# A fourth split slot and later dependent steps in the expert-pair loop of a two-layer transformer trunk

## The reference

```python
logits = (t @ w_router + b_router).astype(jnp.float32)
top_vals, top_idx = lax.top_k(logits, TOP_K)
top_w = jax.nn.softmax(top_vals, axis=-1)
combine = ...                                   # (tokens, 8), two weights per row
for e in range(N_EXPERTS):
    out = out + combine[:, e:e+1] * swiglu(t, w_gate[e], w_up[e], w_down[e])
# swiglu(x) = (silu(x @ w_gate) * (x @ w_up)) @ w_down
# w_gate, w_up: 1024 x 3584, w_down: 3584 x 1024 for each of the 8 experts, all float32
```

## Time and profile before

| | before |
|---|---|
| profiled execution | 1546.36 us |
| its span, first to last instruction | 1544.5 us |
| median of three runs | 1546.59 us |
| PE busy | 1405.0 us (91%) |
| DVE busy | 1282.1 us (83%) |
| ACT busy | 961.6 us (62%) |
| mean DMA rate over the span | 303 GB/s |
| chain that ended last | PE 65%, DVE 16%, issue 10%, ACT 7%, DMA 1% |

### The profile page before, as it was taken

One profiled execution on the slowest core, in us unless ns is written; L12 is line 12 of the kernel. 1 busy time (PEld: TensorE's weight loads), 2 busy tenths in 40 slices (PEclk: granted clock), 3 DMA queues, 4 the chain that ended last, 5 costly groups with the idle time before them and its releaser, 6 DMA issues.

```text
span 1544.5 us, 19314 instructions
## 1 busy us (share of the span) xinstructions
PE 1405.0 (91%) x7122; PEld 1150.3 (74%) x7122; DVE 1282.1 (83%) x1182; ACT 961.6 (62%) x935; POOL 5.6 (0%) x36
## 2 busy tenths in 40 slices
PE   2999799999998699999999999989999998999995
PEld 2877699998877477777777777777777777777774
DVE  6976798886777688889879889888899888898986
ACT  1644443333454367777767777767777777777773
POOL 0000000000000000000000000000000000000000
PEclk9987899998999899999999999999999999999998
DMA  8962389984540489999979999988999988999980
GB/s 332 346 246 83 136 290 342 334 304 164 182 167 1 168 305 370 377 380 377 381 281 354 380 385 375 388 305 311 383 386 382 382 332 296 373 380 385 379 337 29
DMA packets 203949, 467.44 MB, mean 303 GB/s; under 512 B 8734, under 2 KB 10940, under 8 KB 203836
## 3 DMA queue, kind: packets, MB, share of 16 engines
q1 hardware_dynamic: 203836, 465.98, 81.9%
HBM read 464.90 MB, written 1.05 MB: 302 GB/s over the span
## 4 chain that ended last, share of the span: by engine, by line
PE 65%; DVE 16%; issue 10%; ACT 7%; DMA 1%; SPq 0%; DVEq 0%; ACTq 0%
PE bank L1564 16%; PE bank L1566 16%; PE bank L1565 16%; DVE w_lo L1346 10%; ACT w_hi L722 5%; PE bank L1969 3%; PE bank L1886 1%; DVE ring_sum L960 1%; PE bank L1585 1%; PE bank L1607 1%; PE bank L1951 1%; PE bank L1950 1%; PE bank L1895 1%; PE bank L1764 1%; PE bank L1993 1%
## 5 line engine op out<-in xcount | busy, mean ns | idle before, releaser
L1346 DVE TENSOR_TENSOR w_lo<-raw,w_hi 128x2048 fp32r<-128x2048 f32 x336 | 755.8, 2288 | 86.5 <-ACT w_hi L722 86.5
L722 ACT ACTIVATE w_hi<-raw 128x2048 fp32r<-128x2048 f32 x336 | 637.8, 1921 | 143.9 <-PE bank L1566 102.8
L1564 PE MATMUL bank<-w_hi,hg_hi 128*128 128x512 f32 x448 | 183.1, 409 | 19.4 <-DVE w_lo L1346 17.7
L1950 PE MATMUL bank<-w_hi,gs_pack 128*128 128x512 f32 x448 | 180.7, 403 | 10.8 <-DVE w_lo L1346 9.4
L540 ACT ACTIVATE w_hi<-raw 128x2048 fp32r<-128x2048 f32 (+1 forms) x54 | 102.3, 1897 | 130.8 <-PE bank L1566 117.0
L1565 PE MATMUL bank<-w_lo,hg_hi 128*128 128x512 f32 x448 | 177.8, 397 | 0.0
L1566 PE MATMUL bank<-w_hi,hg_lo 128*128 128x512 f32 x448 | 177.7, 397 | 0.0
L1951 PE MATMUL bank<-w_lo,gs_pack 128*128 128x512 f32 x448 | 175.5, 392 | 0.0
L889 DVE TENSOR_TENSOR w_lo<-raw,w_hi 128x2048 fp32r<-128x2048 f32 (+1 forms) x54 | 121.7, 2258 | 19.4 <-ACT w_hi L540 19.2
L1564 PE MATMUL bank<-h_hi,w_hi 128*128 128x256 f32 x448 | 128.2, 286 | 1.6 <-DVE gate_m L938 1.6
L1565 PE MATMUL bank<-h_lo,w_hi 128*128 128x256 f32 x448 | 126.7, 283 | 0.0
(11 more groups left out here) (302 smaller groups left out, 2113.4 us busy)
## 6 DMA issues: line engine op xcount, KB each, us to landing
raw<-in_w_ex_gate SPq DMA_DIRECT2D x112, 1024.0 KB, 6.5
raw<-in_w_ex_up SPq DMA_DIRECT2D x112, 1024.0 KB, 7.2
raw<-in_w_ex_down SPq DMA_DIRECT2D x112, 1024.0 KB, 6.4
raw<-in_w_ada SPq DMA_DIRECT2D x48, 1024.0 KB, 7.2
raw<-in_w_in SPq DMA_DIRECT2D x12, 1024.0 KB, 7.0
raw<-in_w_ff_gate SPq DMA_DIRECT2D x10, 1024.0 KB, 6.5
raw<-in_w_ff_up SPq DMA_DIRECT2D x10, 1024.0 KB, 7.0
raw<-in_w_ff_down SPq DMA_DIRECT2D x10, 1024.0 KB, 6.5
```

What stands on the lines that cost most here:

```text
L722: act_e.activation(w_hi[:, (S0 + n) % SPLIT, :], raw[:, (N0 + n) % RAW, :], ACT.Copy).then_inc(hi_done, 1)
L1346: dve.tensor_tensor(w_lo[:, sl, :], raw[:, (N0 + n) % RAW, :], w_hi[:, sl, :].bitcast(F32), ALU.subtract).then_inc(lo_done, 1)
L1564: mm(o, lh, rh, start=first, stop=False, skip_group_check=True)
L1950: mm(bank[b][:, :], gs_pack[:, kk, :], wh[:, k, :], start=kk == 0, stop=False, skip_group_check=True)
```

## The change

What it does:
- The pair loop gets a fourth slot for `w_hi` and `w_lo` (`more_hi`, `more_lo`, PAIR_SPLIT = 4); the buffers that stood in their place move, `e_hi`, `e_lo` and `f_pack` become single.
- After the router, PE transposes the modulated `hfm` back to token-major rows and ACT writes them over `y` (`modulated_rows`, four copies of 128x512). The gathers then bring rows that are modulated already; ACT takes their high part in one instruction from PSUM (`hg_hi` per half, `gs_pack` at once) and DVE the remainder in one, from PSUM too. `hgf`, `gsf` and the casts go.
- `silu_l(c+1)` and `silu_s(c)` move behind L down half 0 and `gated_s` too, `gated_l` behind S gate half 0, `high_l`, `keep_gate` and `low_l` behind S down half 0, `keep_up` behind the first unit of the next chunk.
- The transposed `e_act` goes to bank 1 in place of bank 0, so that L gate of the next chunk waits for `silu_l` alone and L up for the split; the selection goes to bank 0, a chunk later, and `select` a chunk earlier (chunks 2 and 3).
- ACT at unit n waits for the use of unit n-4.

```diff
-    SEL_L, SEL_S = 3, 4
+    SEL_L, SEL_S = 1, 2
+        pair_hi = [w_hi[:, i, :] for i in range(SPLIT)] + [more_hi[:, :]]
+        pair_lo = [w_lo[:, i, :] for i in range(SPLIT)] + [more_lo[:, :]]
...
+            def modulated_rows():
+
+                for i in range(4):
+                    g, half = i // 2, i % 2
+                    act_e.wait_ge(ym_tp, i + 1)
+                    act_e.activation(y[:, g, half * 512:(half + 1) * 512], bank[i][:, :], ACT.Copy).then_inc(ym_done, 1)
...
                 act_e.wait_ge(hgl_ready, n * 2 + (half + 1))
-                for k in range(4 * half, 4 * half + 4):
-                    modulated(hgf[:, k, :], bank[1 + 2 * half][:, (k % 4) * P:(k % 4 + 1) * P], k, hglf_done)
+                act_e.activation(hg_hi[:, 4 * half:4 * half + 4, :],
+                                 bank[3 * half][:, :].rearrange("p (k t) -> p k t", t=P), ACT.Copy).then_inc(hgl_high, 1)
...
                 act_e.wait_ge(hgs_ready, n + 1)
-                for k in range(KD):
-                    modulated(gsf[:, k, :], bank[3][:, k * HALF:(k + 1) * HALF], k, hgsf_done)
+                act_e.activation(gs_pack[:, :, 0:HALF], bank[3][:, :].rearrange("p (k t) -> p k t", t=HALF),
+                                 ACT.Copy).then_inc(hgs_high, 1)
...
-                    hi_of(j, p * (16 * PU // RAW) + 16 * ((N0 + j) // RAW + 1), p * PU + (S0 + j - SPLIT + 1))
+                    hi_of(j, pair_hi[j % PAIR_SPLIT], p * (16 * PU // RAW) + 16 * ((N0 + j) // RAW + 1),
+                          p * PU + (S0 + j - PAIR_SPLIT + 1))
...
-                    if u[0:2] == ("L", "up") and half == 1:
-                        if c > 0:
-                            silu_s(c - 1)
-                        silu_l(c)
                     if u == ("L", "up", 0, 1):
+                        silu_l(0)
                         evacuate_s(p)
-                    if u == ("L", "gate", 1, 1):
+                    if u == ("S", "up", 0, 1):
+                        keep_gate(0)
+                        high_l(0)
+                    if u == ("L", "gate", 1, 0):
                         keep_up(0)
...
+                    if u[0:2] == ("L", "down") and half == 0 and c < LAST:
+                        silu_l(c + 1)
+                        silu_s(c)
+                    if u[0:2] == ("S", "down") and half == 0 and c < LAST:
+                        keep_gate(c + 1)
+                        high_l(c + 1)
...
+                    if u[0:2] == ("L", "gate") and half == 0 and c > 1:
+                        keep_up(c - 1)
+                    if u == ("S", "down", LAST - 1, 1):
+                        evacuate_l(p + 1, 0)
+                        keep_up(LAST)
...
-                    if u[0:2] == ("L", "down") and half == 1 and c + 1 < EC:
-                        gated_l(c + 1)
-                    if u[0:2] == ("L", "up") and half == 1 and c > 0:
-                        gated_s(c - 1)
-                    if u[0:2] == ("S", "up") and half == 1:
-                        low_l(c)
-                    if u == ("S", "up", LAST, 1):
+                    if u[0:2] == ("S", "gate") and half == 0 and c > 0:
+                        gated_l(c)
+                    if u[0:2] == ("L", "down") and half == 0 and c < LAST:
+                        gated_s(c)
+                    if u == ("S", "up", 0, 1):
+                        low_l(0)
+                    if u[0:2] == ("S", "down") and half == 0 and c < LAST:
+                        low_l(c + 1)
+                    if u == ("S", "down", LAST - 1, 1):
                         split_l(p + 1, 0)
...
+            def rows_of(i):
+
+                g, half = i // 2, i % 2
+                for k in range(4):
+                    last = pe.transpose(bank[i][:, k * P:(k + 1) * P], hfm[:, 4 * half + k, g * P:(g + 1) * P], ident[:, :])
+                last.then_inc(ym_tp, 1)
+
+            rows_of(0)
+            rows_of(1)
             pe.wait_ge(lgt_done, 1)
...
                     if c > 0:
-                        pe.wait_ge(elo_done, p * EC + c)
+                        pe.wait_ge(esilu, p * EC + c)
...
-                    if c == 1:
-                        pe.wait_ge(tl_done, p * 2 + 2)
-                    if c == 2:
-                        pe.wait_ge(ts_done, p * 2 + 2)
+                    if c > 0:
+                        pe.wait_ge(elo_done, p * EC + c)
                     into_l("up", c, 1)
```

More of the change, by code:

```diff
@@ L27 @@
 SPLIT = 3
+PAIR_SPLIT = 4
 UNIT = 2048
@@ L222, in trunk_kernel @@
         late = ExitStack()
[L223 to L228, removed]
+        more_hi = sb("more_hi", [P, UNIT], F32R, where=late)
+        more_lo = sb("more_lo", [P, UNIT], F32R, where=late)
         late.close()
@@ L247, in trunk_kernel @@
         sin2 = sb("sin2", [P, G, 1, RO])
+        summed = ExitStack()
+        g_pre = sb("g_pre", [P, 512], where=summed)
+        u_pre = sb("u_pre", [P, 512], where=summed)
+        summed.close()
         ring_sum = sb("ring_sum", [P, 2, 512])
@@ L295, in trunk_kernel @@
         e_act = sb("e_act", [P, 512], where=moe)
-        e_hi = sb("e_hi", [P, 2, 4, P], F32R, where=moe)
-        e_lo = sb("e_lo", [P, 2, 4, P], F32R, where=moe)
-        hgf = sb("hgf", [P, KD, P], where=moe)
+        e_hi = sb("e_hi", [P, 4, P], F32R, where=moe)
+        e_lo = sb("e_lo", [P, 4, P], F32R, where=moe)
+        f_act = sb("f_act", [P, 4, HALF], where=moe)
+        f_pack = sb("f_pack", [P, 4, P], F32R, where=moe)
+        gs_pack = sb("gs_pack", [P, KD, P], F32R, where=moe)
         hg_hi = sb("hg_hi", [P, KD, P], F32R, where=moe)
@@ L842, in rest_of_expert @@
                             act_e.wait_ge(x_hg_ready, q * 2 + (i + 1))
-                            for k in range(4 * i, 4 * i + 4):
-                                modulated(hgf[:, k, :], bank[6 + i][:, (k % 4) * P:(k % 4 + 1) * P], k, x_hgf)
+                            act_e.activation(hg_hi[:, 4 * i:4 * i + 4, :],
+                                             bank[6 + i][:, :].rearrange("p (k t) -> p k t", t=P), ACT.Copy).then_inc(x_high, 1)
                     if u == ("gate", 0, 1):
@@ L1885, in gather_l @@
                     for g in range(G):
[L1886 removed]
+                        last = mm(bank[3 * half][:, (k % 4) * P:(k % 4 + 1) * P], y[:, g, k * P:(k + 1) * P], sel[:, g, :],
                                   start=(k % 4 == 0 and g == 0), stop=g == 1, skip_group_check=True)
@@ L1945, in into_s @@
                         wh, wl = unit(("S", kind, c, half))
-                        if (kind, c) == ("gate", 0):
-                            pe.wait_ge(hgs_done, p * 4 + (2 * half + 2))
+                        if (kind, c, half) == ("gate", 0, 0):
+                            pe.wait_ge(hgs_done, p + 1)
                         for k in range(4):
@@ L1980, in down_l @@
                                 cs = slice(half * 512, (half + 1) * 512)
-                                last = product(bank[4 + half][:, :], e_hi[:, c % 2, kk, :], e_lo[:, c % 2, kk, :],
+                                last = product(bank[4 + half][:, :], e_hi[:, kk, :], e_lo[:, kk, :],
                                                wh[:, k, cs], wl[:, k, cs], c == 0 and kk == 0, c == LAST and kk == 3)
@@ L1992, in down_s @@
                                 cs = slice(half * 512, (half + 1) * 512)
-                                mm(bank[6 + half][:, :], f_pack[:, c % 2, kk, :], wh[:, k, cs], start=c == 0 and kk == 0,
+                                mm(bank[6 + half][:, :], f_pack[:, kk, :], wh[:, k, cs], start=c == 0 and kk == 0,
                                    stop=False, skip_group_check=True)
-                                last = mm(bank[6 + half][:, :], f_pack[:, c % 2, kk, :], wl[:, k, cs], start=False,
+                                last = mm(bank[6 + half][:, :], f_pack[:, kk, :], wl[:, k, cs], start=False,
                                           stop=c == LAST and kk == 3, skip_group_check=True)
```

122 lines of the change are left out of this document (55 added, 67 removed).

## The result

| | before | after |
|---|---|---|
| median | 1546.48 us (4 runs, 1540.57 to 1547.13) | 1490.17 us (4 runs, 1486.86 to 1493.57) |
| profiled execution, its span | 1546.36, 1544.5 us | 1490.64, 1488.9 us |
| ratio of the times | | 0.9646 (95%: 0.9625 to 0.9668) |

The kernel is 3.5% faster, 56 us. The forecast was 1474 with 1464 to 1515 as the range: the sign and the larger part of the size came as said, 16 us of the gain are missing. The time lies inside the range but above the forecast's own (A, 1464 to 1486), between it and rival B (1500).

The account below looks back on a forecast made before the run. Chunks took 33.2 us, above the PE, DVE and DMA limits, through slot waits, plus boundary stops. DMA-paced landings (unit 331 at 1429), last split at 1446.5, 24.0 us tail and router's 1.1 gave span 1471.6, forecast 1474, range 1464 to 1515.

Parts of the forecast that it names:

- A: Main forecast: DMA sets the pace between boundaries and boundaries shorten; 1474 us, own range 1464 to 1486, chance 0.54.
- rival B: Raw slots don't carry the lag, or PE's clock falls at times; DMA stops at each pair boundary: 1500 us, chance 0.22.
- Three limits, chunk at PE's 30.1 us, then DMA's 32.4: Steady chunk, now 33.2 us: engines alone would need PE's 30.1, so DMA's 32.4 takes over, giving 0.8 us a chunk.
- The fourth slot's lead of 4.2 against 2.9 us: On L units four slots give 4.2 us lead, three give 1.4; PE gains 2.9 on DVE in the S half.
- They add no work: Later steps, other banks and single buffers in the lists: claimed to add no work, with silu_s no longer stopping ACT.
- Gathers, 2.5 to 0.6 us on the path: At gather_s, ACT's copies on the path shrink from 2.5 to 0.6 us; DVE drops four casts per pair.
- Boundary, 53.1 us: Step-by-step walk of the pair boundary: 17 units take 53.1 us instead of 61.3, 8.2 us less.
- The raw slots carry a lag of up to 9.7 us: At boundaries the seven raw slots keep the DMA queue fed up to 9.7 us lag; up to 8 is needed.
- Router, +1.1 us: Ahead of the loop, PE's transposes and ACT's four copies add between 0 and 1.6 us on the path; 1.1 taken.
- Rival D: DMA is at its limit already, by contention with the engines; only trifles stay, 1542 to 1550 us, chance 0.08.
- Rival C: Fourth slot doesn't even out L and S; chunk stays at 33.2 us, only boundaries gain: 1514 us, chance 0.10.
- Rival E: PE standing at S units lowers its clock, each fall costing 1.7 us; three falls a chunk give 1610 us, chance 0.06.

## Why the prediction came out as it did

*Three limits, chunk at PE's 30.1 us, then DMA's 32.4: right.* Behind a boundary the chunks are 30.4 to 30.9, at the end of a pair 31.9. DMA's limit was set 1.7% too slow: my 2.705 us a unit came from a window of 40 us ahead of the experts, while in the loop gate and up units land 2.71 us apart and down units 2.56, 2.66 on average, 31.9 us for 12.

*The fourth slot's lead of 4.2 against 2.9 us: right, but not enough by itself.* Without the later places the slot gave 14 us. The step that failed in the text is "They add no work": a step that makes ACT wait for PE takes from the same 4.2 us. I had costed ACT's stops at nothing because the ledger was one of work. Before had one at the fold in every chunk, 69.3 us in all, where after has 23.4:

```profile
ACT f_act L781 <- PE bank L1969: 69.3, 28, 2.6
```

The forecast's total held only because both parts were made together.

*Gathers, 2.5 to 0.6 us on the path: not seen.* With PE's jump in the kernel the difference is none. It is still part of the walk that came out at 53.1, but no run isolates it there.

*Boundary, 53.1 us: the failed step.* It says "L gate 0 at 14.7": PE starts the next pair as soon as its unit is split. PE stands 4.45 us at the jump and then runs 3.4 to 6.8 us at half clock, which costs half of that: 4.45 + 3.4 = 7.9 at the first boundary, 4.3 + 1.7 = 6.0 at the others. Measured over the walk are 60.4 - 53.1 = 7.3, then 5.9 and 5.7. In before the sign of it was in the trace: PE idle for 3.15 us, of which the split, ready 2.5 us ahead of PE's start, explains 0.7. I read the name behind the arrow instead of the end of the row that it names.

*The raw slots carry a lag of up to 9.7 us: right in part, and the total by luck.* The walk's boundary lags 53.1 - 17 x 2.66 = 7.9 us behind DMA. With PE's loop written out the loop takes 907.2 us, 1.4 more than the forecast's 905.8 (541.8 to 1447.6), which looks as if nothing were lost. Two errors cancel in it. At 2.71 and 2.56 us a unit, 84 units need 223.4 us, not the 227 of the forecast. But from one boundary to the next that kernel takes 227.3 and 227.0 us: its five chunks behind a boundary win back 4.9 of the 7.9 us, and 3.6 to 3.9 a pair are lost. The rate of 375 GB/s around its boundary and landings up to 4.8 us apart show the same. In after the jump adds its 7 us, and the first boundary has a gap of 7.0 us between two landings, the others of 4.9 and 5.0. This is rival B's mechanism, in a small part there without the jump and made larger by a stop that B didn't name.

*Router, +1.1 us: wrong, nothing.* From DVE's copy of the logits to the first split of the loop it was 15.3 us before and 14.8 after. The first split ends at 536.2, 5.6 us sooner than the forecast's 541.8, and that is no gain of the change: between two executions with the same code ahead of the loop it moves by 3.5 us (540.7 in before, 537.2 with PE written out in before), and among the kernels with the change from 534.4 to 542.8. In the sum these 5.6 us are luck.

*The sum.* Forecast span 1471.6. Start of the loop -5.6, the loop 928.0 against 905.8, +22.2 (of which 20.8 are the jump, by the written-out kernel's 907.2, and 1.4 everything else), the tail 24.7 against 24.0, +0.7: 1488.9.

*The rule of the Trainium skill.* "DMA: Bandwidth & Descriptors", "Where 436 GB/s comes from", has HBM to SBUF bound near 358 GB/s, which it gets by halving a stack's 716 GB/s between two cores; this kernel runs on one. The trace disagrees more than before: 395 GB/s over 151 us of the loop. Rival D, which had the same result, is out with it.

*Rival C* (chunk stays at 33.2) is what the chunks do with either half of the change on its own, at 1529 and 1538 us for its 1514, since their boundaries (58.7 to 61.6 and 60.0 to 62.1 us) gave little of the 8.2 us either. *Rival E* didn't occur: in the middle of pairs, where DMA sets the pace, the granted clock is 1.00.

The version that beats both is after with PE's loop written out, 1470.0 us, 4.7% below before. With all three engines written out it is 1468.0; the 2 us between them are too few to tell.

## What to carry to other kernels

Lead from more buffers is spent by every wait in the same in-order list, so cost the waits of a moved step together with the slots, and try each alone before crediting one. When a chain is shortened, ask what was hidden beside it: look for idle time whose named releaser had long ended, above all where an engine's loop jumps back, and on every engine. If taking a stop away gives nothing, look whether another engine has the same stop next to it. A walk of the boundary done agreed within 0.2 us at the steps compared, once the one unmodelled stop was removed, so such a walk is worth its length; a total that agrees isn't enough, as two terms of this one cancelled.

## What the runs showed of the hardware

- PE stands 4.30 to 4.45 us at its jump back to the loop's head, with data and slot ready, and then runs 3.4 or 6.8 us at 1.2 GHz. Writing PE's loop out took 20 us off (1490.17 to 1470.02). In every such stop of after one 16 KB packet runs on an instruction queue, and PE starts 1.7 to 1.8 us after its end.
- ACT's jump can stop it too: 4.16 us at the second boundary of before with PE written out. In the changed kernel ACT's and DVE's jumps cost nothing that could be told (1467.99 against 1470.02 us).
- The same stop can be put down to another engine in the profile: 3.15 us "for DVE" in before, of which DVE's row explains 0.7.
- Units of 1 MiB land 2.71 us apart for gate and up and 2.56 for down, whose rows in HBM are 4 KB long against 2 KB. 395 GB/s held for 151 us with PE, DVE and ACT all at work.
- The granted clock fell to the lower level at PE's stops of 4.3 to 4.45 us at each jump of after, and at two of the three stops of 2.02 us behind a boundary in the kernel with chunk 0's steps later. It stayed at the third of these, at stops of 1.23 us, and at the 3.15 us in before, whose one fall at that boundary (3.4 us from 766.2) began as PE went on after a stop of 2.08 us.
